# A decoder trunk in one launch: the last attention units of layer 1 are issued in another order

## What is computed

```python
proj = h @ b_w_in[l - N_A_LAYERS]
q_dil, q_mem = jnp.split(proj, [DIL_QK_WIDTH], axis=-1)
q_dil = partial_rope(q_dil.reshape(B, S, n_dil, HEAD_DIM), cos, sin)
mix = dilated_mixture(q_dil, shared_k, shared_v)      # 3 groups of 12 heads, windowed softmax attention
mo = memory_attention(q_mem.reshape(B, S, MEM_HEADS, HEAD_DIM), mkv[:, :, 0], mkv[:, :, 1])
x = x + jnp.concatenate([mix, mo], axis=-1) @ w_out[l]
x = x + peer(rmsnorm(x, norm_ffn[l]), peer_wq[l], peer_keys[l], peer_u[l], peer_v[l])
...
# inside one attention branch
s = jnp.where(valid, einsum('...qc,...kc->...qk', qb, kc) * HEAD_DIM ** -0.5, -jnp.inf)
m = jnp.max(s, axis=-1, keepdims=True)
e = jnp.exp(s - m)
den = jnp.sum(e, axis=-1, keepdims=True)
o = einsum('...qk,...kc->...qc', e / den, vc)
```

## Time and profile before

| | us |
|---|---|
| median of 3 runs | 3196.49 (3196.42 to 3196.59) |
| the profiled execution's own time | 3195.37 |
| its span in the trace | 3193.6 |
| PE busy in the span | 3150.6 (99%) |
| DVE busy | 2545.1 (80%) |
| ACT busy | 1636.8 (51%) |
| POOL busy | 1020.8 (32%) |

### The profile page before, as it was taken

The page is one execution under the profiler, slowest core; times in us unless marked ns, Lnnn a source line. Parts: engine busy times, 40 slices in busy tenths (PEclk is TensorE's granted clock), DMA queues, the critical chain, the costliest instruction groups (busy, mean ns, idle before and its releaser), DMA issues.

```text
span 3193.6 us, 48756 instructions
## 1 busy us (share of the span) xinstructions
PE 3150.6 (99%) x17822; PEld 2817.2 (88%) x17822; DVE 2545.1 (80%) x5378; ACT 1636.8 (51%) x3053; POOL 1020.8 (32%) x626
## 2 busy tenths in 40 slices
PE   8999999999999999999999989999999999999999
PEld 7878899999998888888978868899999998888887
DVE  5685898989857988885378876898989866888886
ACT  5343249696943333335255654248686853333333
POOL 1001464545422444520000000354445432444440
PEclk9999999999999999999999999999999999999999
DMA  5123269898999999993222214259898998999994
GB/s 199 44 66 118 85 222 349 308 351 303 354 366 340 379 391 390 396 367 115 68 86 74 87 61 138 81 171 337 314 346 312 345 383 315 374 401 398 389 392 146
DMA packets 324925, 827.33 MB, mean 259 GB/s; under 512 B 26064, under 2 KB 158672, under 8 KB 317520
## 3 DMA queue, kind: packets, MB, share of 16 engines
q1 hardware_dynamic: 250960, 555.75, 48.5%
q0 software_dynamic: 73728, 268.47, 22.5%
HBM read 718.16 MB, written 105.96 MB: 258 GB/s over the span
## 4 chain that ended last, share of the span: by engine, by line
PE 43%; DVE 3%; DMA 2%; ACT 1%; issue 1%; SPq 0%; DVEq 0%; ACTq 0%
PE p_bank L2346 16%; PE p1r_h_ps L2282 16%; PE ba_bank L416 6%; PE o_bank L1753 1%; DMA hiddens<-p_h_sb 1%; PE p1r_gate_ps L2330 1%; PE ba_oT_ps L476 1%; PE ba_t_ps L497 1%; PE p1r_s_ps L2306 0%; PE ba_s_ps L439 0%; DVE p_grow L2711 0%; DVE ba_e L644 0%; ACT p1r_cols L2452 0%; PE ba_s_ps L444 0%; DMA raw<-in_u 0%
## 5 line engine op out<-in xcount | busy, mean ns | idle before, releaser
L2413 ACT ACTIVATE peer_hi<-raw 128x1024 fp32r<-128x1024 f32 x540 | 570.9, 1057 | 673.9 <-PE p_bank L2346 604.3
L2703 DVE TENSOR_TENSOR peer_lo<-raw,peer_hi 128x1024 fp32r<-128x1024 f32 x434 | 530.0, 1223 | 308.1 <-ACT peer_hi L2413 307.3
L2244 POOL TENSOR_TENSOR peer_lo<-raw,peer_hi 128x1024 fp32r<-128x1024 f32 x106 | 263.3, 2485 | 1083.2 <-ACT peer_hi L2413 1083.1
L2256 POOL DMA_INDIRECT p_grow<-in_v_rows,p_expert x256 | 388.6, 1518 | 468.9 <-DVE p_acc L2720 384.1
L2256 POOL DMA_INDIRECT p_grow<-in_u_rows,p_expert x256 | 359.2, 1403 | 506.8 <-DVE p_hid L2711 479.2
L2346 PE MATMUL p_bank<-peer_hi,p_w_hi 128*128 128x512 f32 x1500 | 461.8, 389 | 0.0
L2346 PE MATMUL p_bank<-peer_hi,p_w_lo 128*128 128x512 f32 x1500 | 461.8, 389 | 0.0
L2346 PE MATMUL p_bank<-peer_lo,p_w_hi 128*128 128x512 f32 x1500 | 461.7, 389 | 0.0
L2282 PE MATMUL p1r_h_ps<-h_hi,peer_hi 128*128 128x384 f32 (+2 forms) x1152 | 396.9, 345 | 1.3 <-ACT p_h_sb L2431 0.9
L2282 PE MATMUL p0r_h_ps<-h_hi,peer_hi 128*128 128x384 f32 (+2 forms) x1152 | 396.7, 344 | 0.6 <-DVE peer_lo L2703 0.5
L2282 PE MATMUL p1r_h_ps<-h_lo,peer_hi 128*128 128x384 f32 (+2 forms) x1152 | 391.4, 340 | 0.0
(11 more groups left out here) (438 smaller groups left out, 5531.9 us busy)
## 6 DMA issues: line engine op xcount, KB each, us to landing
raw<-in_u SPq DMA_DIRECT2D x256, 512.0 KB, 6.1
raw<-in_v SPq DMA_DIRECT2D x256, 512.0 KB, 8.3
p_g_sb<-gates SPq DMA_DIRECT2D x64, 768.0 KB, 11.1
hiddens<-p_h_sb SPq DMA_DIRECT2D x240, 192.0 KB, 4.7
p_w_raw<-hiddens SPq DMA_DIRECT2D x60, 768.0 KB, 7.5
gates<-x SPq DMA_DIRECT2D x24, 1024.0 KB, 9.7
raw<-in_w_b_mix SPq DMA_DIRECT2D x38, 512.0 KB, 3.5
raw<-in_w_peer_q SPq DMA_DIRECT2D x32, 512.0 KB, 3.6
```

The source lines that it names most:

```text
L2244: pool.tensor_tensor(lo[:, m % NH, :], raw[:, m % NR, :], hi[:, m % NH, :].bitcast(F32), ALU.subtract).then_inc(lo_pool, 1)
L2256: pool.indirect_dma_start(out=grow[:, g % RG, :], out_offset=None, in_=table, in_offset=bass.IndirectOffsetOnAxis(ap=expert[:, at:at + 1], ...
L2413: act.activation(hi[:, n % NH, :], raw[:, n % NR, :], ACT.Copy).then_inc(hi_ready, 1)
L2703: dve.tensor_tensor(lo[:, m % NH, :], raw[:, m % NR, :], hi[:, m % NH, :].bitcast(F32), ALU.subtract).then_inc(lo_dve, 1)
```

## The change

Three edits in the attention of layer 1 and one in the output projection:

1. On PE, from step 23 on, `turn(s-1)` stands at the head of the step, ahead of `output(s-2)`; before, it stood at its end. In step 22, `scores(22)` stands ahead of `output(20)`, and `scores(23)` right behind it.
2. `scores(22)`, `scores(24)` and `scores(26)` now go to `bank`, and 23, 25 and 27 to `s_ps`; before, it was the other way round. So `scores(22)` waits for `bank` to be read by `halves(37)`, and no longer for `maximum(21)`.
3. On DVE, in step 22, `sines(37)` and `rotate(37)` stand ahead of `maximum(21)` and `finish(18)`.
4. `turn_o(0)` to `turn_o(2)` of layer 1 use other PSUM banks, since the last unit's scores lie elsewhere.

No instruction is added or taken away, and no DMA is moved in SP's list.

```diff
-            t = bank if n >= DENSE and (n - DENSE) % 2 else s_ps
+            t = bank if n >= DENSE and (n - DENSE) % 2 == 0 else s_ps
...
-                if n == DENSE + 1:
+                if n == DENSE:
                     pe.wait_ge(bank_free, TILES)
...
             for s in range(UNITS + 3):
                 for K in range(first_step(s), first_step(s + 1)):
                     product(K)
+                if s == DENSE:
+                    scores(s)
+                if DENSE < s and s - 1 < UNITS:
+                    turn(s - 1)
                 if 0 <= s - 2 < UNITS:
                     output(s - 2)
                 if s < DENSE:
                     scores(s)
+                if s == DENSE:
+                    scores(s + 1)
                 if 0 <= s - 3 < UNITS - 1:
                     turn_back(s - 3)
                 if DENSE < s < UNITS - 1:
                     scores(s + 1)
-                if 0 <= s - 1 < UNITS:
+                if 0 <= s - 1 and s <= DENSE:
                     turn(s - 1)
-                if s == DENSE:
-                    scores(s)
-                    scores(s + 1)
...
                 if s == DENSE:
                     halves(TILES - 1)
+                    sines(TILES - 1)
+                    rotate(TILES - 1)
                 if 0 <= s - 1 < DENSE:
                     maximum(s - 1)
...
                 if s == DENSE:
-                    sines(TILES - 1)
-                    rotate(TILES - 1)
                     maximum(s)
...
-            return t_ps[:, (k + 2) % BANKS, :]
+            return t_ps[:, (k + (0 if strided else 2)) % BANKS, :]
```

## The result

19 runs of each kernel, on one chip: 3202.24 us with the change (3196.20 to 3208.93) against 3196.15 before (3193.27 to 3206.12), ratio 1.0016 with a 95% interval of 1.001 to 1.0022 (3.2 to 7.0 us). The change makes the kernel slower, by 6 us there. The forecast was 3196.7, no change, at most 3199.4.

A forecast was written before the change was run, and what follows sets the result against it. PE, busy in 99% of the span, was taken as the bound. Steps gained about 0.4 us each, less a clock fall and 1.7 us in the tail: first output product +0.2 us, median 3196.7, range 3194.2 to 3199.4.

The forecast's parts named there:

- The walk: Forecast start times from `scores(22)` through `turn(27)` to the first output product, put at 1921.9 us against 1921.75 before.
- The clock decides the next part: Step 22: PE's clock falls in the 4.5 us break; 3.4 us at half speed taken, middle of none and 6.8.
- The second rival: Clock stays low for 6.8 us, 3198.4, or falls again, 3200.2; chance 0.2.
- the idle time from 91.7 to 94.7: PE idle while ACT does unit 22's exponentials (times less 1800); a second clock fall there adds up to 1.8 us.
- The tail gives it back: Last unit: `output(27)` comes 3.85 us after `turn(27)` where it was 2.15, so 1.7 us are lost.
- The sum: First output product +0.2 us, profiled execution 3195.6, median 3196.7, made against the profiled execution of the kernel before.
- The lead of 2.9 us at `turn(23)`: Unit 23's transposes were to start 2.9 us earlier than the 1901.43 of before; the lead shrinks to 1.5 at `turn(27)`.
- Periods: Steady steps of the attention: period falls from 4.68 to about 4.27 us, PE waiting ahead of `turn` for ACT's move.
- Clock not lost: Rival at step 22: clock stays up or returns at once, saving 1.5 us at half speed, 3195.2; chance 0.15.
- PE's own 3.4 us a period: Rival: periods from `turn(22)` to `turn(27)` fall to PE's own work, gaining 6.4 us, 3190.1; chance 0.05.
- The fourth rival: DVE's `shift` or its DMA comes last, `turn(27)` keeps its time, only the tail's 1.7 us added, 3198.2; chance 0.06.
- The factor of half speed: PE's transposes and scores at step 22 take 1.8 to 2 times as long at the lower clock.

The follow-up runs named there:

- filled: Changed kernel plus idle identity transposes in its three long PE breaks; 3198.07 us, ratio 0.9998 to the kernel before, stretch 43.89 us.
- filled_tail: Changed kernel, three PE breaks filled with idle transposes, and ACT's move of unit 27 ahead of copy 26; 3197.49 us, ratio 0.9994 to before.
- before_filled: Kernel before plus 24 idle transposes behind `output(20)`, in its one long PE break; 3194.76 us, ratio 0.9987, stretch 42.89 us.
- step22_filled: Kernel before with only the step 22 edits, plus 28 idle transposes ahead of `scores(22)`; 3193.27 us, ratio 0.9985, stretch 42.22 us.
- late_filled: Step 22 edits with 28 idle transposes, and `turn` ahead of `output` in steps 24 to 27 only; 3197.22 us, ratio 0.9995 to before.
- tail_old: Changed kernel with `turn(27)` back in its old place behind `output(26)` and its turn-back; 3202.61 us, ratio 1.0012 to before, stretch 48.43 us.
- again: Changed kernel measured and profiled once more, no edit; 3201.59 us, ratio 1.0005 to the kernel before, stretch 48.92 us.

## Why the prediction was wrong

- **The walk was nearly right in its order and distances.** The order of events, the releasers and the starts up to `turn(27)` came within 0.4 us in the first profile, and at full clock the stretch is 43.89 where the walk gives 43.2. (The 42.5 for before and the 42.3 for step 22 alone, measured 42.89 and 42.22, were worked out after the result.) That the first profile matched so well as far as `turn(27)` was luck: its first fall lasted just the 3.4 us at half speed that had been taken as the middle of two bounds.
- **The step that failed is the paragraph "The clock decides the next part".** There I took one fall of 3.4 us at half speed, the middle between none and 6.8. Each of the four profiles with the change has a second fall and one a third; the first fall lasted 3.4 us in two of them and 6.8 in the others, and all together 6.8 to 13.7, 11 on average. The walk's stretch is 44.7 us, that is 43.2 and 1.5 for the clock. Measured were 48.06, that is 43.89 and 4.2 for the clock. So of the 3.4 us that the forecast is short, 2.7 are this term and 0.7 the walk itself.
- The second rival had this mechanism, priced at 3198.4 for a long fall and 3200.2 for a second one, and I gave it 0.2. It should have been the forecast, though 3200.2 is still 2 us under the median of 3202.24. The prediction names the idle time from 91.7 to 94.7, which is longer than the break that had cost the kernel before its clock (2.72 us), and prices it as a rival only; the break of 2.2 us ahead of `turn(27)` it doesn't price at all.
- The rule of the Trainium skill (TensorE: Matmul & The Clock Gate, section What's actually happening) that the low clock is the default and that activity lifts it spoke against the change, and was right. The trace agrees: in the five profiles whose long breaks were filled with idle work (filled, filled_tail, before_filled, step22_filled, late_filled) no fall is left in the stretch.
- **"The tail gives it back"** was right in its distance (3.91 us from `turn(27)` to `output(27)`, 3.85 forecast). The 1.7 us are no cost to be won back, though: `turn(27)` itself stands nearer to the move of unit 26 in the new order (1.18 us behind it in filled, 2.40 before), and from that move on the tail takes 5.09 against 4.55, so 0.5 us. The sum has both sides and isn't wrong by it; what I expected of tail_old was.
- **The lead of 2.9 us at `turn(23)`** was read at the instruction that had been moved. At ACT's move of unit 22, which both orders need, the walk's lead is 0.5 us (1897.4 against 1897.9), and at full clock there is none (19.05 against 19.03). The lead that the new order then builds, 1.0 us at unit 25, ends at the wait for DVE's `shift`, as the table above shows.
- **Periods:** 4.33 on average from `turn(23)` to `turn(26)` (1899.80 to 1912.79, three periods), 4.27 forecast. PE waits ahead of `turn` for ACT's move, as forecast. The gain of 0.4 a step is there and doesn't reach the end: late_filled against step22_filled.
- **Clock not lost, and PE's own 3.4 us a period:** neither happened. The fourth rival, `shift` as the last to come, didn't happen as priced either, since `turn(27)` came 1.2 us earlier (1917.91 less 1.16, against 1917.95). But the wait that it names is there, and it hangs on `scores(27)`, not on a DMA (DVE reaches `shift` without an idle gap): ACT stands idle for it for 1.90 us in the changed kernel and for 0.45 before. The row of the changed kernel's first profile, to be held against the first of the earlier trace rows:

```profile
1914.54 0.22 ACT L568 ACTIVATE layer_share<-layer_below 128x16 f32<-128x16 f32 x1 [1.90 <-DVE layer_below L681]
```

- **The factor of half speed**, "1.8 to 2" in the prediction, is 2.2 and 1.7 by the four numbers beside it (1.90 against 0.87, 1.87 against 1.07). Nothing in the sum changes by it.
- **The measure:** the sum was held against three runs that lay within 0.2 us. Nineteen lay within 13. The three profiles of the kernel before have equal stretches (44.58 to 44.71) and took 3195.37, 3196.87 and 3199.59, so this spread arises outside of it. The median of the kernel before also moved between the measurements, from 3196.15 to 3199.57; a range of 5 us was narrow whatever the mechanism.

What stays open: 3.4 us of longer stretch stand against 6.1 us in the medians of the first measurement and 2.0 in those of the second. They lie inside both intervals (3.2 to 7.0 us, and 1.3 less to 4.5 more), so nothing has to be missing. What lies behind the stretch is 1268.7 to 1275.2 us with the change and 1271.8 to 1276.0 before, with no sign that the change makes it longer; ahead of it are 1874.7 to 1879.0 and 1877.1 to 1878.0. So I put the rest down to the spread of the runs, without having shown it.

## What to carry to other kernels

An engine's break costs more than its length where its clock follows its work. Before moving a wait, list all breaks of PE in the new order, those off the path too, and compare each with the breaks that already cost the clock in the trace. A shorter one isn't safe by that: 2.2 us was below anything that had cost the clock before, and six of eleven such breaks did. Where a break can't be avoided, idle products into a free bank, placed behind a wait that is over anyway, keep the clock up. Here they took 1.8 us off the stretch of the kernel before, 2.3 with the edits of step 22 and 4.2 with the changed order, while the best order alone took off 0.7 (42.89 to 42.22 at full clock).

A lead in the middle of a pipeline is worth nothing if its last stages wait for another engine in both orders. So measure a lead at an instruction that wasn't moved, and follow the last unit's own inputs: what was moved ahead of them delays them.

## What the runs showed of the hardware

- In the stretch of all 18 profiles the clock fell to half speed (1.2 instead of 2.4 GHz) within, or up to 1.5 us behind, each of the eight breaks of 4.4 to 4.7 us on PE and each of the four of 2.7 to 3.0 that lie at `turn_back(19)`, and five of the seven of 3.0 to 3.1 ahead of `turn(22)`. Of eleven breaks between 2.1 and 2.5 us six had a fall, and breaks of 1.8 us and less had none. That each fall is counted to the break just ahead is a reading of the order in time. The stretches at half speed lasted 3.4, 6.8 or 10.2 us, also within one kernel.
- A fall doesn't wait for the longest idle time. In the run again the clock fell 0.7 us before the end of a 4.39 us break (0.53 granted in the microsecond from 1883). It came back at 1889.9, while PE worked without a break from 1883.8 to 1891.1, and fell again 2.2 us into the next break, at 1893.3.
- 28 transposes of 128 x 128 in a row took 3.28 us, 0.12 each, and were enough to hold the clock through a break of 4.5 us of which they left 1.1 and 0.4 us empty.
